# Branch products from split operands, gate inputs read back in eight transfers, and another order of VectorE's work

## The chip, the cores and the metric

One core of a Trainium2 (trn2) chip runs the whole program in one launch. The metric is the device time in microseconds (us); lower is better.

## The reference

Two layers of a block with four parallel token-mixing branches and a gated feed-forward part, over 256 context tokens and 256 latent tokens of width 1024. What matters here is the merge of the branches:

```python
def merge_branches(h, ys, w_branch, w_gate, b_gate, w_o):
    gates = jax.nn.sigmoid(h @ w_gate + b_gate)
    acc = gates[..., :D_MODEL] * (ys[0] @ w_branch[0])
    for i in range(1, N_BRANCH):
        acc = acc + gates[..., i * D_MODEL:(i + 1) * D_MODEL] * (ys[i] @ w_branch[i])
    return acc @ w_o
```

Branches 0 to 3 are a short gated convolution, neighbourhood attention, grouped-query attention and a two-pass RWKV-7 recurrence, each 256 channels wide. After the merge come an RMS norm, a residual sum, a second RMS norm with modulation, and the feed-forward part. In layer 1 only the latent tokens go through the merge and what follows.

## The kernel before

Everything is held with channels on the 128 partitions and tokens along the free axis, 512 columns (T) in layer 0 and, for most products, 256 in layer 1. A product of a weight with an activation is made by `project` (L2109): ACT rounds a weight half (1024 x 128) to fp32r (`whi`, L988), DVE takes the rest (`wlo = ring - whi`, L1472), the activation is held as a high and a low part as well, and PE makes three matmuls for each 128 rows: high x high, high x low, low x high (L2118 to L2120). The halves are made `SPLIT` = 3 ahead, in a ring of three slots for each of whi and wlo; SP's queue loads the blocks of two halves (1 MB each) into a ring of three as `lo_done` or the product frees a slot. The branch products (L2508) are the exception: they read the branch outputs `YB` and the weights `WB` as plain fp32, two matmuls for each output tile of 128 channels.

The order of PE's jobs is written out once in `job_list` (L213); each job takes the next PSUM bank in turn (`bank_plan`, L282) and waits until that bank's last user has read it. The stages of one layer in order, with the layer-0 times of the profile:

- Attention in steps of two units (to 318 us). In each step come scores, transposes, some of the gate products (branches 0 and 1, `gates_in_step`) and preparatory work of the recurrence (`first_pass`). In the step `PREP_STEP[l]["shift"]` DVE finishes three shifted copies (`shifted`, L1639) that ACT begins (L1109) at the end of its own step; DVE's `first_pass` stands ahead of its `split_until` for the step's gates.
- The two passes of the recurrence (318 to 455 us): products of small blocks, then the levels 2, 4, 8, 16, 32 of a triangular inverse, each of jobs `sx`, `tt`, `sy` (L2365, L2353, L2405) with extras (`tok` L2316, `xv` L2397), then `u0` and `at` (L2416, L2424), then a chunk loop with modulation jobs (`mod` L2165, `modt` L2173), then `y1` and `y23` (L2466, L2478, L2482). In the second pass POOL brings the gate inputs `HG` back from DRAM (L914): after `tok k` it issues two transfers of 2 MB (1 MB in layer 1), one for the high and one for the low part. At the end DVE makes three wlo halves (L1472), then adds `y1` (L1882) and `y23` (L1890) into YB.
- The merge loop (455 to 604 us). For J in 0 to 3, two output tiles j at a time, the branches go in `GATE_ORDER` = 2, 0, 1, 3; branches 2 and 3 have their gate products here (48 matmuls for the two tiles), those of 0 and 1 come back from DRAM as `GB`. The recurrence's group norm is worked in at J = 0 (`mean`, `var`, `g2`: L2499, L2515, L2521; `centred`, `readout`). POOL loads WB (1 MB for each J, two buffers, L922), GB (L927), and at J = 1 the residual stream X (L934). In layer 0 ACT squares X (`XX`) and DVE sums the squares during J = 2 and 3.
- The output product (`wo`, 604 to 649 us), 24 matmuls for each of eight tiles. Layer 0 is `FUSED`: while wo runs, ACT and DVE form squares and sums (L1960, L1963, L1968), and four `sum` jobs (L2527, L2536, L2538, L2541) give both norms at once. `sum 0` (the sum of XX) stands ahead of the last wo tile.
- The gap (649 to 663 us): four modulation jobs on PE, the roots on ACT, then for each tile on DVE `scaled_out` (L1988), `new_x` (L1993), `normed` (L1997), on ACT the modulated value (L1396) and its high part (L1400), on DVE `low` (L2001). Then `project_first` (L2127; matmuls L2141 to L2143) starts five up tiles side by side, 15 matmuls for each tile of the input as it comes.

What sets the start of the first late gate product is this part of DVE's order:

```python
if d == 1:
    split_until(half_no(("gate", l, 0, GATE_ORDER[0])) + SPLIT)
```

## Time and profile before

| what | value |
|---|---|
| median of 3 runs | 1687.19 us (1682.79 to 1688.15) |
| the profiled execution | 1686.72 us |
| its span | 1684.9 us |
| PE / PEld / DVE / ACT / POOL busy | 1603.2 / 1317.8 / 912.0 / 780.8 / 302.5 us |
| mean granted TensorE clock | 0.978 |
| bytes moved | 234.41 MB, mean 139 GB/s |

The profiled execution took 1686.72 us by the device's count, 1.8 us more than the span of its records, and lies 0.5 us under the median. PE is TensorE's matmuls, PEld its weight loads, DVE VectorE, ACT ScalarE, POOL GpSimd, SP SyncE (only DMA issues). A matmul's recorded length is modelled and overlaps the next one's, so the pace is read from start to start. PEclk 1.00 stands for 2.4 GHz and 0.50 for 1.2 GHz. "issue" is time in which an engine waited for nothing that the profile shows. An fp32 matmul has two records, an fp32r one has one.

### The profile page before, as it was taken

The page shows a single profiled execution, that of the slowest core. Times are in us where ns is not written, and L with a number is a line of the kernel's source. Part 1 is how long each engine was busy: PE and PEld are TensorE (multiplying, and loading weights), DVE is VectorE, ACT ScalarE, POOL GpSimd, SP SyncE. Part 2 cuts the span into 40 slices and gives each one's busy share as a digit, 9 for nine tenths or more (in the row PEclk, how much of TensorE's full clock was granted, in tenths as well). Part 3 has the DMA queues.
Part 4 walks back from the last instruction along what each step waited for, and adds up shares of the span by engine and source line. Part 5 has one row for each costly group of instructions (what it writes and reads, how often), then busy time and mean ns, then how long its engine had stood idle before and what let it go on. Part 6 is the DMA issues. An engine that isn't in the chain of part 4 may idle for free.

```text
span 1684.9 us, 33073 instructions
## 1 busy us (share of the span) xinstructions
PE 1603.2 (95%) x14128; PEld 1317.8 (78%) x14128; DVE 912.0 (54%) x1457; ACT 780.8 (46%) x1295; POOL 302.5 (18%) x241
## 2 busy tenths in 40 slices
PE   6999999998899999999999998999998899999997
PEld 3788767777766676888888885987876789899997
DVE  3264455564344558555554225655776356567754
ACT  4332456473343346534434225525666444566652
POOL 0160234322010000111222000211452020012201
PEclk8999999998999999999999999999999999999999
DMA  9753234233862252123324434833413384544553
GB/s 336 185 159 99 95 107 157 73 114 93 276 221 79 75 175 75 54 97 101 100 88 94 113 111 139 256 125 113 131 63 128 94 296 161 198 154 163 178 173 116
DMA packets 230497, 234.41 MB, mean 139 GB/s; under 512 B 5904, under 2 KB 217232, under 8 KB 230352
## 3 DMA queue, kind: packets, MB, share of 16 engines
q1 hardware_dynamic: 210720, 190.09, 34.7%
q0 software_dynamic: 15024, 35.92, 7.8%
q10 hardware_dynamic: 4608, 6.29, 1.1%
q8 instruction: 113, 1.85, 0.4%
q14 instruction: 32, 0.26, 0.1%
HBM read 216.55 MB, written 15.73 MB: 138 GB/s over the span
## 4 chain that ended last, share of the span: by engine, by line
PE 72%; DVE 4%; issue 2%; ACT 2%; DMA 1%; POOL 0%; ACTq 0%; DVEq 0%; POOLq 0%
PE ps L2118 17%; PE ps L2119 16%; PE ps L2120 16%; PE ps L2508 5%; PE ps L2165 2%; PE ps L2365 2%; PE ps L2353 1%; PE ps L2405 1%; PE ps L2141 1%; PE ps L2142 1%; PE ps L2143 1%; PE ps L2327 1%; PE ps L2173 1%; DVE wlo L1472 1%; PE ps L2316 1%
## 5 line engine op out<-in xcount | busy, mean ns | idle before, releaser
L988 ACT ACTIVATE whi<-ring 128x1024 fp32r<-128x1024 f32 (+1 forms) x264 | 274.9, 1045 | 512.2 <-PE ps L2120 467.8
L1472 DVE TENSOR_TENSOR wlo<-ring,whi 128x1024 fp32r<-128x1024 f32 (+1 forms) x264 | 327.4, 1245 | 182.5 <-ACT whi L988 181.9
L2118 PE MATMUL ps<-H,whi 128*128 128x256 f32 (+1 forms) x640 | 215.1, 336 | 1.9 <-DVE wlo L1472 1.8
L2120 PE MATMUL ps<-H,wlo 128*128 128x256 f32 (+1 forms) x640 | 214.9, 336 | 0.0
L2119 PE MATMUL ps<-H,whi 128*128 128x256 f32 (+1 forms) x640 | 214.8, 336 | 0.0
L2118 PE MATMUL ps<-HR,whi 128*128 128x512 f32 (+1 forms) x568 | 203.0, 357 | 3.4 <-DVE wlo L1472 3.4
L2120 PE MATMUL ps<-HR,wlo 128*128 128x512 f32 (+1 forms) x568 | 199.0, 350 | 0.0
L2119 PE MATMUL ps<-HR,whi 128*128 128x512 f32 (+1 forms) x568 | 198.9, 350 | 0.0
L2118 PEld LDWEIGHTS ps<-H,whi 128*128 128x128 f32 x640 | 122.2, 191 | 14.5 <-issue 2.2
L2120 PEld LDWEIGHTS ps<-H,wlo 128*128 128x128 f32 x640 | 122.2, 191 | 12.2
L2119 PEld LDWEIGHTS ps<-H,whi 128*128 128x128 f32 x640 | 122.3, 191 | 12.0
L2118 PEld LDWEIGHTS ps<-HR,whi 128*128 128x128 f32 x568 | 108.2, 191 | 20.7 <-issue 7.1
L2119 PEld LDWEIGHTS ps<-HR,whi 128*128 128x128 f32 x568 | 108.2, 191 | 14.3 <-issue 1.0
L2120 PEld LDWEIGHTS ps<-HR,wlo 128*128 128x128 f32 x568 | 108.2, 190 | 13.9
L886 POOL TENSOR_SCALAR pr<-pr,stat 128x512 f32<-128x512 f32 (+1 forms) x48 | 72.1, 1514 | 237.3 <-DVE stat L1744 237.3
L2118 PE MATMUL ps<-UA,whi 128*128 128x512 f32 (+1 forms) x320 | 107.6, 336 | 0.0
L2119 PE MATMUL ps<-UA,whi 128*128 128x512 f32 (+1 forms) x320 | 107.5, 336 | 0.0
L2120 PE MATMUL ps<-UA,wlo 128*128 128x512 f32 (+1 forms) x320 | 107.5, 336 | 0.0
L942 POOL TENSOR_TENSOR CU<-CU,rs 128x512 f32<-128x512 f32 (+1 forms) x22 | 39.3, 1786 | 367.8 <-ACT rs L1440 367.8
L2118 PE MATMUL ps<-HG,whi 128*128 128x512 f32 (+1 forms) x256 | 91.1, 356 | 4.5 <-DVE YB L1882 4.5
L2120 PE MATMUL ps<-HG,wlo 128*128 128x512 f32 (+1 forms) x256 | 86.8, 339 | 0.0
L2119 PE MATMUL ps<-HG,whi 128*128 128x512 f32 (+1 forms) x256 | 86.7, 339 | 0.0
(351 smaller groups left out, 3076.6 us busy)
## 6 DMA issues: line engine op xcount, KB each, us to landing
ring<-in_ffn_up SPq DMA_DIRECT2D x44, 1024.0 KB, 5.0
ring<-in_w_gate SPq DMA_DIRECT2D x32, 1024.0 KB, 5.7
ring<-in_ada_w SPq DMA_DIRECT2D x32, 1024.0 KB, 5.1
ring<-in_w_in SPq DMA_DIRECT2D x24, 1024.0 KB, 6.6
ring<-in_ffn_down SPq DMA_DIRECT2D x32, 512.0 KB, 3.7
ada<-in_ada_w SPq DMA_DIRECT2D x8, 1024.0 KB, 11.6
WB<-in_w_branch POOLq DMA_DIRECT2D x8, 1024.0 KB, 6.8
ring<-in_w_o SPq DMA_DIRECT2D x8, 1024.0 KB, 5.0
```

What stands on the lines that cost most here:

```text
L886: pool.tensor_scalar(pr[:, u % 4, 0:nk], pr[:, u % 4, 0:nk], stat[:, 2, u % 4:u % 4 + 1], None, ALU.mult).then_inc(p_ready, 1)
L942: pool.tensor_tensor(u, u, (rs, rt)[j % 2][:, c0:c1], ALU.mult).then_inc(u_ready, 1)
L988: act.activation(whi[HALF_SLOT[m]][:, 0:kn, :], ring[:, SLOT[raw] % RING, 0:kn, P * half:P * half + P], ACT.Copy).then_inc(hi_done, 1)
L1472: dve.tensor_tensor(wlo[HALF_SLOT[m]][:, 0:kn, :], ring[:, SLOT[raw] % RING, 0:kn, P * half:P * half + P], whi[HALF_SLOT[m]][:, 0:kn, :].b ...
L2118: pe.matmul(o[:, c0:c1], hi[:, i, :], part(0, k), start=(k == 0), stop=False)
L2119: pe.matmul(o[:, c0:c1], hi[:, i, :], part(1, k), start=False, stop=False)
L2120: last = pe.matmul(o[:, c0:c1], lo[:, i, :], part(0, k), start=False, stop=(k == kn - 1))
L2141: pe.matmul(o, hi[:, k, :], part(0, k)[:, c0:c1], start=(k == 0), stop=False)
L2142: pe.matmul(o, hi[:, k, :], part(1, k)[:, c0:c1], start=False, stop=False)
L2165: last = pe.matmul(o[STRIP * g:STRIP * g + STRIP, 0:SLOT_N], cpad[:, k, :], w[:, k, :], start=(k < STRIPS), stop=(k >= KT - STRIPS))
L2365: last = pe.matmul(o[side(y), x, CH2 * b:CH2 * b + CH2].rearrange("k (g n) -> k g n", n=z), LM1[side(x), 2 * p + y, b, 0:CH], even_blocks( ...
L2508: last = pe.matmul(o[:, c0:c1], wb[:, 2 * i + k, P * (j % 2):P * (j % 2) + P], YB[:, 2 * i + k, c0:c1], start=(k == 0), stop=(k == 1))
```

## The change

- The branch products of layer 0 (`BRANCH_SPLIT`) are made like the others, from high and low parts: ACT rounds branch outputs (`YH`, `source_hi`, eight of 128 x 512) and branch weights (`WH`, three slots, `branch_hi`, eight of 128 x 1024), DVE takes the low parts (`YL`, `WL`), PE makes six fp32r matmuls for a job that had two fp32 ones. `YH` lies where X is, so X is read back in four transfers behind the last branch products, and the squares of X with their sums move into the wo loop.
- The gate inputs come back in eight transfers (0.5 MB each in layer 0, 0.25 MB in layer 1), each behind another job of the second pass's levels (`GATE_INPUT_BEHIND`), in both layers.
- `sum 0` moves behind the other three sums.
- DVE: in the shift step the halves come ahead of `first_pass`; at the end of the second pass one half, `y1` of pair 0, one half, `y1` of pair 1, one half; in the layer-0 gap `normed` of the next tile stands ahead of `low`, and `low(0)` ahead of the modulation sum.
- ACT: in the layer-0 gap the row copy of the last modulation job comes behind the first tile's high part.

```diff
+SOURCE_ORDER = [2 * i + x for i in GATE_ORDER for x in range(2)]
...
+GATE_INPUT_BEHIND = [("tok", "k", 1), ("sx", 16, 1), ("tt", 16, 1), ("sy", 16, 1),
+                     ("sx", 32, 1), ("tt", 32, 1), ("sy", 32, 1), ("u0", 1)]
...
+BRANCH_SPLIT = (0,)
...
-jobs += [("wo", l, j) for j in range(7)] + [("sum", l, 0)] * (l in FUSED) + [("wo", l, 7)]
+jobs += [("wo", l, j) for j in range(8)]
 if l in FUSED:
-    jobs += [("sum", l, q) for q in range(1, 4)] + FILL.get(("gap", l, 1), []) + FILL.get(("gap", l, 2), [])
+    jobs += [("sum", l, q) for q in (1, 2, 3, 0)] + FILL.get(("gap", l, 1), []) + FILL.get(("gap", l, 2), [])
...
+YH = at("YH", 0, [KT, T], F32R)
+YL = at("YL", 16, [KT, T], F32R)
+WH = at("WH", 156, [3, KT, P], F32R)
+WL = at("WL", 112, [2, KT, SLOT_N], F32R)
...
-for part in range(2):
-    pool.dma_start(HG[:, part, :, c0:T], hsave[part, :, c0:T].rearrange("(k p) t -> p k t", p=P))\
+for n, behind in enumerate(GATE_INPUT_BEHIND):
+    pool.wait_ge(mm_done, done_at((behind[0], l, 1) + behind[1:]))
+    part, k = n // 4, n % 4 * 2
+    pool.dma_start(HG[:, part, k:k + 2, c0:T],
+                   hsave[part, P * k:P * k + 2 * P, c0:T].rearrange("(k p) t -> p k t", p=P))\
         .then_inc(h_back[l], 16)
...
-if J == 1:
...
-        if l:
-            pool.wait_ge(x_saved, 16)
-        pool.dma_start(X[:, :, c0:c1],
-                       (xsave if l else a["xin"])[:, c0:c1].rearrange("(k p) t -> p k t", p=P))\
-            .then_inc(x_back, 16)
+    if J == 1 and l not in BRANCH_SPLIT:
+        pool.wait_ge(x_saved, 16)
+        pool.dma_start(X[:, :, c0:c1], xsave[:, c0:c1].rearrange("(k p) t -> p k t", p=P))\
+            .then_inc(x_back[0], 16)
     pool.wait_ge(wb_in, 16 * (4 * l + J + 1))
+if l in BRANCH_SPLIT:
+    for i in GATE_ORDER:
+        pool.wait_ge(mm_done, done_at(("br", l, KT - 1, i)))
+        pool.dma_start(X[:, 2 * i:2 * i + 2, c0:c1],
+                       a["xin"][2 * P * i:2 * P * i + 2 * P, c0:c1].rearrange("(k p) t -> p k t", p=P))\
+            .then_inc(x_back[i], 16)
...
+def fill(point, part=slice(None)):
+    for job in [job for job in FILL.get(point, []) if job[0] == "mod"][part]:
...
+def source_hi(n):
+    act.activation(YH[:, n, c0:c1], YB[:, n, c0:c1], ACT.Copy).then_inc(yh_done, 1)
+def branch_hi(j):
+    act.wait_ge(wb_in, 16 * (4 * l + j // 2 + 1))
+    if j > 2:
+        act.wait_ge(mm_done, done_at(("br", l, j - 3, GATE_ORDER[3])))
+    act.activation(WH[:, j % 3, :, :], WB[:, j // 2 % 2, :, P * (j % 2):P * (j % 2) + P], ACT.Copy)\
+       .then_inc(wh_done, 1)
+if l in BRANCH_SPLIT:
+    act.wait_ge(ya_ready, 2 * l + 2)
+    for n in range(len(units) - NBANK, len(units)):
+        emptied(act, ("PV", l, n))
+    act.wait_ge(mm_done, done_at(("y23", l, 1, 1)))
+    for i in GATE_ORDER[:3]:
+        for n in (2 * i, 2 * i + 1):
+            source_hi(n)
...
    .then_inc(frees(("gate", l, j, i)), 1)
+if l in BRANCH_SPLIT and (j, i) == (0, GATE_ORDER[0]):
+    branch_hi(0)
+    branch_hi(1)
...
-if l in FUSED and J >= 2:
-    n = 4 * (J - 2) + GATE_ORDER.index(i)
-    if n == 0:
-        act.wait_ge(x_back, 16 * (l + 1))
-    if n > 1:
-        act.wait_ge(x2_added, 7 * FUSED.index(l) + n - 1)
-    act.activation(XX[:, min(n, 1), c0:c1], X[:, n, c0:c1], ACT.Square).then_inc(x2_ready, 1)
+if l in BRANCH_SPLIT:
+    if i == GATE_ORDER[2] and J < 3:
+        branch_hi(2 * J + 2)
+    if READOUT.get((J, i)) == "g2":
+        for p in range(2):
+            emptied(act, ("g2", l, p))
+            source_hi(6 + p)
+    if i == GATE_ORDER[3] and J < 3:
+        branch_hi(2 * J + 3)
...
 for j in range(KT):
+    act.wait_ge(x_back[j // 2], 16)
+    if j > 1:
+        act.wait_ge(x2_added, 7 * f + j - 1)
+    act.activation(XX[:, min(j, 1), c0:c1], X[:, j, c0:c1], ACT.Square).then_inc(x2_ready, 1)
     s = filled(act, ("wo", l, j))
...
-fill(("gap", l, 2))
+fill(("gap", l, 2), slice(0, 1))
...
 act.activation(H2[:, 0, i, c0:c1], OB[:, i, c0:c1], ACT.Copy).then_inc(h_hi, 1)
+if i == 0:
+    fill(("gap", l, 2), slice(1, None))
...
-first_pass(j // 2)
+shift_step = j // 2 == PREP_STEP[l]["shift"]
+if not shift_step:
+    first_pass(j // 2)
 for t in gates_in_step(l, j // 2):
     name = ("gate", l) + t
     split_until(min(half_no(name), half_no(("gate", l) + GATE_TILES[-1]) + 1 - SPLIT) + SPLIT)
+if shift_step:
+    first_pass(j // 2)
...
+first_gate = half_no(("gate", l, 0, GATE_ORDER[0]))
 if d == 1:
-    split_until(half_no(("gate", l, 0, GATE_ORDER[0])) + SPLIT)
+    split_until(first_gate + 1)
...
 ins.then_inc(frees(("y1", l, d, p)), 1)
+split_until(first_gate + p + 2)
...
+def source_lo(n):
+    dve.wait_ge(yh_done, 8 * BRANCH_SPLIT.index(l) + SOURCE_ORDER.index(n) + 1)
+    dve.tensor_tensor(YL[:, n, c0:c1], YB[:, n, c0:c1], YH[:, n, c0:c1].bitcast(F32), ALU.subtract)\
+       .then_inc(yl_done, 1)
+def branch_lo(j):
+    dve.wait_ge(wh_done, 8 * BRANCH_SPLIT.index(l) + j + 1)
+    half = slice(P * (j % 2), P * (j % 2) + P)
+    dve.tensor_tensor(WL[:, j // 2 % 2, :, half], WB[:, j // 2 % 2, :, half],
+                      WH[:, j % 3, :, :].bitcast(F32), ALU.subtract).then_inc(wl_done, 1)
+if l in BRANCH_SPLIT:
+    for n in SOURCE_ORDER[:6]:
+        source_lo(n)
+    branch_lo(0)
+    branch_lo(1)
...
-if l in FUSED and J >= 2:
-    n = 4 * (J - 2) + GATE_ORDER.index(i)
-    dve.wait_ge(x2_ready, 8 * FUSED.index(l) + n + 1)
-    if n:
-        if n > 1:
-            dve.wait_ge(x2_added, 7 * FUSED.index(l) + n - 1)
-        dve.tensor_tensor(XX[:, 0, c0:c1], XX[:, 0, c0:c1], XX[:, 1, c0:c1], ALU.add).then_inc(x2_added, 1)
+if l in BRANCH_SPLIT:
+    if READOUT.get((J, i)) == "g2":
+        for p in range(2):
+            emptied(dve, ("g2", l, p))
+            source_lo(6 + p)
+    if i == GATE_ORDER[2] and J < 3:
+        branch_lo(2 * J + 2)
+    if i == GATE_ORDER[3] and J < 3:
+        branch_lo(2 * J + 3)
...
-dve.wait_ge(x_back, 16 * (l + 1))
 for j in range(KT):
     t = tile_of_sums(j)
+    dve.wait_ge(x2_ready, 8 * f + j + 1)
+    if j:
+        if j > 1:
+            dve.wait_ge(x2_added, 7 * f + j - 1)
+        dve.tensor_tensor(XX[:, 0, c0:c1], XX[:, 0, c0:c1], XX[:, 1, c0:c1], ALU.add).then_inc(x2_added, 1)
+    dve.wait_ge(x_back[j // 2], 16)
...
 dve.wait_ge(root_ready, norm_no(l, 2) + 1)
+normed(0)
 for i in range(KT):
-    normed(i)
-    if i:
-        low(i - 1)
-    else:
+    if i + 1 < KT:
+        scaled_out(i + 1)
+        new_x(i + 1)
+        normed(i + 1)
+    low(i)
+    if i == 0:
         fill(("gap", l, 2))
-        scaled_out(1)
-    if i + 1 < KT:
-        new_x(i + 1)
-    if i + 2 < KT:
-        scaled_out(i + 2)
-low(KT - 1)
...
-pe.wait_ge(h_back[l], 32)
+pe.wait_ge(h_back[l], 128)
...
-for j in (2 * J, 2 * J + 1):
+for j in (2 * J, 2 * J + 1) if l in BRANCH_SPLIT else ():
+    o = job(("br", l, j, i))[:, c0:c1]
+    f = 8 * BRANCH_SPLIT.index(l)
+    pe.wait_ge(yl_done, f + 2 * GATE_ORDER.index(i) + 2)
+    pe.wait_ge(wl_done, f + j + 1)
+    half = slice(P * (j % 2), P * (j % 2) + P)
+    for k in (2 * i, 2 * i + 1):
+        pe.matmul(o, WH[:, j % 3, k, :], YH[:, k, c0:c1], start=(k == 2 * i), stop=False)
+        pe.matmul(o, WH[:, j % 3, k, :], YL[:, k, c0:c1], start=False, stop=False)
+        last = pe.matmul(o, WL[:, J % 2, k, half], YH[:, k, c0:c1], start=False, stop=(k > 2 * i))
+    done(last)
...
-if j == KT - 1 and l in FUSED:
-    pe.wait_ge(x2_added, 7 * (FUSED.index(l) + 1))
-    o = job(("sum", l, 0))
-    done(pe.matmul(o[:, c0:c1], K("ones"), XX[:, 0, c0:c1], start=True, stop=True))
...
+pe.wait_ge(x2_added, 7 * (f + 1))
+o = job(("sum", l, 0))[:, c0:c1]
+done(pe.matmul(o, K("ones"), XX[:, 0, c0:c1], start=True, stop=True))
```

## Rows read from the trace of the kernel before

**Rows 1.** The page: busy time of each engine.
```profile
PE 1603.2 (95%) x14128; PEld 1317.8 (78%) x14128; DVE 912.0 (54%) x1457; ACT 780.8 (46%) x1295; POOL 302.5 (18%) x241
```

**Rows 2.** The chain in layer 0's merge loop: start, length, what.
```profile
494.41 3.43 PE ps L2508 x8
508.74 10.30 PE ps L2508 x24
```

**Rows 3.** Engines in one whole J of that loop (stretch: length, busy PE, PEld, DVE, ACT, POOL, PEclk, DMA share, GB/s).
```profile
533.36:568.88 35.52, 35.52 (x130) 24.10 (x129) 16.52 (x23) 12.44 (x19) 0.89 (x1) 1.00 0.26 89
```

**Rows 4.** Groups by shape: DVE's and ACT's work on a weight half.
```profile
L1472 DVE TENSOR_TENSOR wlo<-ring,whi 128x1024 fp32r<-128x1024 f32 x248 | 312.0, 1264 | 155.2 <-ACT whi L988 154.6
L988 ACT ACTIVATE whi<-ring 128x1024 fp32r<-128x1024 f32 x248 | 261.4, 1058 | 474.1 <-PE ps L2120 438.0 <-PE ps L2143 7.1 <-PE ps L2196 6.4
```

**Rows 5.** Timeline of DVE in the wo loop, layer 0: the least idle time.
```profile
643.89 0.69 DVE L1960 TENSOR_TENSOR SQB<-X,OB 128x512 f32<-128x512 f32 x1 [0.61 <-ACT OB L1373]
```

**Rows 6.** Windows as in rows 3: levels of layer 0, gate start of layer 1.
```profile
416.00:418.00 2.00, 0.01 (x1) 0.01 (x1) 0.00 (x0) 0.00 (x0) 0.00 (x0) 1.00 1.07 317
418.00:420.00 2.00, 2.00 (x79) 1.83 (x79) 0.42 (x1) 0.60 (x1) 0.03 (x1) 0.76 0.12 32
...
422.00:424.00 2.00, 2.00 (x20) 1.67 (x23) 0.33 (x1) 0.82 (x2) 0.00 (x0) 0.50 1.01 211
...
1362.00:1364.00 2.00, 2.00 (x11) 2.00 (x11) 0.00 (x0) 0.00 (x0) 0.00 (x0) 0.50 1.08 388
```

**Rows 7.** The chain through levels 16 and 32 of the second pass, both layers.
```profile
411.84 1.29 PE ps L2365 x64
...
428.36 0.27 PE ps L2416
...
1320.70 1.05 PE ps L2365 x45
...
1326.30 0.55 PE ps L2365 x32
...
1330.13 1.93 issue
...
1334.48 1.92 PE ps L2416 x64
```

**Rows 8.** PE's first gate matmul in either layer, and the first branch products of layer 1.
```profile
456.86 0.47 PE L2118 MATMUL ps<-HG,whi 128*128 128x512 f32 x1 [1.93 <-DVE YB L1882]
1360.34 0.36 PE L2118 MATMUL ps<-HG,whi 128*128 128x256 f32 x1 [2.53 <-DVE YB L1882]
1368.68 3.45 PE ps L2508 x16
```

**Rows 9.** POOL's queue at the same place: its wait for the first WB of each layer.
```profile
462.01 0.90 POOL L922 DMA_DIRECT2D WB<-in_w_branch  x1 [4.35 <-DMA WB<-in_w_branch]
1367.34 0.89 POOL L922 DMA_DIRECT2D WB<-in_w_branch  x1 [6.80 <-DMA WB<-in_w_branch]
```

**Rows 10.** The gap of layer 0: DVE, ACT, PE's chain, and the clock.
```profile
657.57 0.69 DVE L1997 TENSOR_TENSOR OB<-X,SQB 128x512 f32<-128x512 f32 x1 [0.21 <-ACT SQB L1388]
658.90 0.38 ACT L1001 ACTIVATE mrow<-ps 128x256 f32<-128x256 f32 x1 [1.15 <-PE ps L2165]
662.02 0.68 DVE L2001 TENSOR_TENSOR H<-OB,H 128x512 fp32r<-128x512 f32 x1
662.85 0.77 PE ps L2141
666.00:668.00 2.00, 2.00 (x6) 1.61 (x5) 2.00 (x4) 1.34 (x3) 0.00 (x0) 0.50 0.00 0
668.00:670.00 2.00, 2.00 (x9) 1.57 (x9) 2.00 (x5) 1.32 (x4) 0.00 (x0) 0.95 0.00 0
```

**Rows 11.** The shift step of layer 1: timeline of PE and of DVE.
```profile
1165.16 0.36 PE L2118 MATMUL ps<-HR,whi 128*128 128x256 f32 x1 [3.09 <-DVE wlo L1472]
1161.81 0.75 DVE L1639 SCALAR_TENSOR_TENSOR lora<-Z,vec,lora 128x510 f32<-128x510 f32 x1 [3.17 <-ACT lora L1109]
```

11 lines of the change are left out of this document (7 added, 4 removed).

## The prediction

> **What bounds the kernel now.** I read the page first: PE is busy 95% of the span [rows 1]. So time can go in two ways only: less work on PE where it never waits, or shorter waits in the places where it does. The merge loop of layer 0 is of the first kind. One J takes 35.52 us, PE is busy in all of it at clock 1.00, while DVE works 16.52 and ACT 12.44 us [rows 3]. The chain there is PE alone: two branch jobs take 3.43 us [rows 2], and the 48 gate matmuls between 497.84 (494.41 + 3.43) and 508.74 take 10.90 us, 0.227 us each. The places of the second kind are four: the levels of the second pass, the first late gate product after it, the gap of layer 0, and the shift step of layer 1 [rows 6 to 8, 10, 11]. Everything else (attention apart from that step, feed-forward, layer 1's merge loop) is left as it is.
>
> **The change part by part.** The sum is made against the profiled execution's own 1686.72 us, which lies 0.5 us under the median of 1687.19; I let that half microsecond go.
>
> *Branch products, layer 0.* Now a job is two fp32 matmuls, 3.43 / 2 = 1.715 us [rows 2]. It becomes six fp32r matmuls of the gate products' shape: 6 x 0.227 = 1.36 us. There are 8 tiles x 4 branches = 32 jobs: 32 x 0.353 = 11.3 us less PE. What is added elsewhere: for each J two weight halves more on ACT (2 x 1.06 us) and on DVE (2 x 1.26 us) [rows 4], which makes DVE about 19 and ACT about 15 of the new 32.7 us, so PE hides them; cost 0 as long as order and latency allow. The late one is `branch_hi(2J+3)`, which waits for the first of the last two branch jobs of J; from there ACT 1.06, DVE's last multiplies and adds (some four of 0.69 [rows 5]) and 1.26 make about 5 us, and its reader stands behind 10.9 us of gates. At the head of the loop the sources come first (six of about 0.6 on ACT, of 0.69 on DVE), then WB, which landed at 462.0 [rows 9], then 1.06 + 1.26: the first low part is there near 464.5, and the gates and the mean keep PE until about 467. Cost 0; if WB came 3 us later, PE would stand that much. I count **-11.2**.
>
> *X and its squares.* The transfer of X leaves a busy stretch of the DMA and comes back as four of 0.5 MB behind the last branch jobs; the first squares are wanted some 14 us after the first of them is issued, and the last pair some 30 us after. Cost 0. In the wo loop DVE gets one addition of 0.69 us a tile. Its least idle time there is 0.61 us [rows 5], so it is full for two or three tiles and may end a few tenths late: the cover is nearly gone. `sum 0` takes the same 0.86 us of PE behind the other sums as ahead of the last tile; the sums that ACT and DVE wait for come earlier by that much, but ACT then waits for PE's second modulation job, whose time is the same. I count **0**, bounds -0.8 and +1.
>
> *Gate inputs.* In layer 0 PE stood in the middle of one job, where it waits for no semaphore, while DMA was full (1.07 in 416 to 418), and went on when the transfer was over (0.12 in 418 to 420); then the clock was 0.50 [rows 6]. I read this as PE's instructions coming late behind the 2 MB. From the start of `sx 16` to the start of `u0` took 428.36 - 411.84 = 16.5 us. Layer 1 has one undisturbed level, 1326.30 - 1320.70 = 5.6 us, and a last one of 8.18 us with 1.93 of the same wait in it, so 6.25 without [rows 7]: 11.9 together, a gain of 4.7 in layer 0. In layer 1 it is the 1.93 and about 0.9 of half clock in `u0` (1.92 us long), 2.8. A transfer of a quarter of the size can still hold one fetch up by a quarter of the time, so I take 4.0 and 2.5, together **-6.5**. Bounds: 0 (the fetches are as late as before) and -8. POOL issues eight instead of two and has nothing else until `y23`; the last, behind `u0`, is issued about 25 us before its reader. The Trainium skill, page "DMA: Bandwidth & Descriptors", section "Queues, rings and completion order", says that each DMA engine takes turns between the queues it has work for, a packet at a time; by that rule an instruction fetch would not wait for a whole transfer of another queue, however large, and the eight would bring nothing. The wait of [rows 6] that ended with the transfer speaks against it.
>
> *The first late gate product.* Before, DVE makes three halves and then adds `y1`, for whose bank PE waits: 1.93 us in layer 0, 2.53 in layer 1 [rows 8]. Now one half (1.26) and two additions stand ahead of it, both shorter than PE's `y23`, so PE goes straight on. Layer 0: **-1.9**. In layer 1 the 2.5 us, and some 1.7 lost to the half clock that followed (0.50 in 1362 to 1364 [rows 6]), bring PE sooner to its branch products; but WB landed at 1367.3 and the products began at 1368.68 [rows 8, 9]. More than 1.3 is not to be had, PE then stands about 2.5 us for WB, and the clock may fall again. I take **-0.5**, bounds -1.3 and +0.5.
>
> *The gap of layer 0.* `normed(0)` begins at 657.57, `low(0)` at 662.02, and PE starts at 662.85 [rows 10]. Between them stand the modulation sum and ACT's row copy at 658.90, which waits for PE and holds up the first modulated value. Afterwards: ACT starts at 658.3 (1.1 + 0.6), DVE makes three operations of 0.6 meanwhile, `low(0)` ends near 660.9, PE starts at 661.05: 1.8 less. PE then has been idle 1.7 instead of 3.5 us. It ran at 0.50 until about 668.2 (0.95 in 668 to 670), 5.4 us, and at full speed half of that, 2.7, is saved if the clock stays up. It stayed up after the idle 1.93 of layer 0's gate start and fell after the 2.53 of layer 1's [rows 6, 8]. DVE makes a tile in 4 x 0.6 = 2.4 us and PE uses one in 15 x 0.227 = 3.4, so DVE isn't late next. **-4.4**, bounds -1 and -4.6.
>
> *The shift step.* In layer 1 DVE waited 3.17 us for ACT's copies with two halves behind them, and PE 3.09 us for the first of these halves [rows 11]. Now the halves go first; ACT made the second by 1160.2, so both are ready by 1161.5, when PE wants them. DVE's later work moves by 2.1 us only (the copies themselves are no earlier), and that governs the rest of the step: **-2.3**, bounds 0 (another engine takes over) and -3.1. In layer 0 PE did not wait there: **-0.3** for less crowding on DVE.
>
> Sum: 11.2 + 6.5 + 1.9 + 0.5 + 4.4 + 2.3 + 0.3 = 27.1. 1686.7 - 27.1 = **1659.6**.
>
> **The rivals.**
> - *The transfers do not matter.* The stalls stay (by whatever cause, the page's turn-taking among them). Then 6.5 is missing: 1666. For it: similar waits named "issue" are seen without traffic. Against: the end of the wait with the end of the transfer.
> - *The clock takes part back.* It falls in the gap of layer 0 all the same (+2.7) and while PE waits for WB in layer 1 (+1): 1663. Speaking for it: the light modulation jobs ahead of the gap; against: the 1.93 us that did no harm.
> - *The split branch products are fed late.* The first pair waits for WB, ACT, DVE, or each J waits for the half behind the last branch job, 2 to 3 us each: about 1669. Against it stand the 5 us of margin worked out above.
> - *The change doesn't do what it says.* The fp32r branch matmuls keep a pace of 0.29 us (1.715 / 6), as they alternate between tiles of several buffers: 1671. No row shows this, every fp32r product here runs at 0.227.
> - *Slower: each small transfer stalls PE.* If a transfer of any size cost a stall of about 2.9 us, as the one in layer 0 did, then 16 transfers instead of four would mean up to 12 stalls more, 35 us, in the levels of both layers, and the 6.5 would not come either: 1686.7 - 20.6 + 35 = 1701. It decides from about seven more stalls on. Against it: one of the two transfers of layer 0 did nothing of the sort.
>
> **How the numbers follow.** Forecast 0.52, clock 0.16, transfers 0.14, fed late 0.08, not as it says 0.03, slower 0.03, and 0.04 for several terms falling short together (about 1675). About 0.3% (5 us) is what a measurement of this kernel can tell from no change; all cases but one lie well under 1682, so faster 0.95, same 0.02, slower 0.03. The range goes up to 1671, over the first four cases. Down, if all terms reached their bounds (0.8 + 1.5 + 0.8 + 0.2 + 0.8), it would be 1655.5; new overlap in places that I have not priced takes it to 1652.
>
> **What would show it.** Layer 0's J should take 32.7 us with L2508 gone from it and matmuls of WH, WL at 0.227. No idle time of PE within one job in levels 16 and 32, clock 1.00 there; `sx 16` to `u0` near 12 us. PE's first HG matmul directly behind `y23` in both layers; in layer 1 a wait for WB ahead of the first L2508. PEclk 1.00 from the first H2 matmul on. No wait of 3 us in layer 1's shift step. I am wrong on the main term if a J takes over 34 us; wrong on the transfers if waits called issue of over 1 us stand in the middle of a job.

## The result, and the profile after

| kernel | median | runs | ratio to before, 95% interval |
|---|---|---|---|
| before | 1686.2 us | 4 (1682.79 to 1688.15) | |
| changed, first comparison | 1668.95 us | 4 (1663.82 to 1778.68) | 0.988 [0.985, 0.9911] |
| before, repeated | 1689.06 us | 17 (1684.0 to 1700.02) | |
| changed, repeated | 1667.7 us | 6 (1663.49 to 1682.34) | 0.9877 [0.9838, 0.9915] |

The changed kernel is about 1.2% faster. The forecast was 1659.6 us with 1652 to 1671 around it: the sign and the range hold, the point lies 8 to 9 us too low. The profile read here is that of the repeat, because in the first profile of the changed kernel, the run of 1778.68 us, TensorE had only 0.85 of its clock. The execution of the repeat's profile took 1670.02 us, its span 1668.2 us: 16.7 less than the span of before.

In the changed kernel the branch products are L2585 to L2587 (layer 0) and L2592 (layer 1), the fp32r products of `project` L2191 to L2193, of `project_first` L2214 to L2216, a level's `sx`, `tt`, `sy` L2438, L2426, L2478.

The page, engine times as in [rows 1], and one row of its queue part (packets, MB, share of 16 engines) that will matter:

```profile
PE 1589.0 (95%) x14192; PEld 1325.5 (79%) x14192; DVE 926.5 (56%) x1473; ACT 792.3 (47%) x1311; POOL 312.5 (19%) x256
...
q8 instruction: 114, 1.87, 0.5%
```

PE's busy time is 14.2 us shorter. The second row is PE's program itself: it is read in packets of 16 KB while the kernel runs.

Windows, columns as in [rows 3]: a whole J of layer 0, the levels, the chunk loop behind them, the gap.

```profile
525.14:557.78 32.64, 32.64 (x145) 27.04 (x144) 17.38 (x23) 12.17 (x17) 0.88 (x1) 1.00 0.29 97
416.00:418.00 2.00, 0.59 (x9) 0.56 (x10) 0.23 (x1) 0.00 (x0) 0.00 (x0) 0.96 0.96 237
418.00:420.00 2.00, 2.00 (x28) 1.67 (x30) 0.20 (x1) 1.08 (x2) 0.93 (x2) 0.50 0.37 82
440.00:442.00 2.00, 0.98 (x16) 0.42 (x16) 0.37 (x2) 0.00 (x0) 0.00 (x0) 0.93 1.08 366
442.00:444.00 2.00, 2.00 (x24) 1.64 (x20) 0.29 (x1) 0.38 (x1) 0.00 (x0) 0.50 1.08 376
648.00:650.00 2.00, 2.00 (x6) 1.61 (x5) 1.95 (x4) 0.96 (x3) 0.00 (x0) 0.50 0.04 8
```

J takes 32.64 us where [rows 3] had 35.52, and PE is full in it. But the levels still have their hole (416 to 418) with the half clock behind it, and two more things go against the forecast: half clock in the chunk loop, where before ran at 1.00, and half clock after the gap.

PE's timeline at the places of [rows 6, 8, 10] and in the chunk loop (start, length, what, idle time before it and what ended it):

```profile
417.40 0.31 PE L2438 MATMUL ps<-TN,LM 64*64 64x32 f32 x6 [2.16 <-issue]
437.01 1.07 PE L2238 MATMUL ps<-ring,cpad 128*32 128x256 f32 x16 [0.34 <-DMA ring<-in_ada_w]
441.02 1.29 PE L2238 MATMUL ps<-ring,cpad 128*32 128x256 f32 x16 [1.41 <-DMA ring<-in_ada_w]
647.39 0.77 PE L2214 MATMUL ps<-H,whi 128*128 128x512 f32 x1 [1.89 <-DVE H L2077]
1341.02 0.36 PE L2191 MATMUL ps<-HG,whi 128*128 128x256 f32 x1 [0.33 <-DVE wlo L1519]
1350.50 0.92 PE L2592 MATMUL ps<-YB,WB 128*128 128x256 f32 x3 [2.64 <-DMA WB<-in_w_branch]
```

The wait of 2.94 us inside a job has become 2.16. The modulation jobs of the chunk loop (L2238) wait for their weights, which they did nowhere in this loop before. The idle time of the gap went from 3.48 to 1.89. The first late gate product of layer 1 follows at once (2.53 before), and PE waits 2.64 for WB ahead of the first branch product, as forecast (2.5).

DVE in the shift step of layer 1, where before had the 3.17 us of [rows 11]: the halves come first.

```profile
1145.20 1.22 DVE L1519 TENSOR_TENSOR wlo<-ring,whi 128x1024 fp32r<-128x1024 f32 x1 [0.46 <-ACT whi L1006]
1146.75 0.75 DVE L1686 SCALAR_TENSOR_TENSOR lora<-Z,vec,lora 128x510 f32<-128x510 f32 x1 [0.33 <-ACT lora L1127]
```

Since both kernels issue nearly the same matmuls in the same order, each can be matched with its own in the other trace; the difference of the start times, read at the borders of the stages, splits the 16.7 us:

```
stage (times of before)                        forecast   measured
start, attention, first pass (0 to 399)          -0.3       -2.8   (shift step of layer 0: -1.1; clock about -1.1)
second pass, layer 0 (399 to 454)                -4.0       +2.3
first late gate product, layer 0                 -1.9       -1.9
merge loop, layer 0 (457 to 605)                -11.2      -11.4
wo and gap, layer 0 (605 to 672)                 -4.4       -1.4
shift step, layer 1                              -2.3       -2.6
rest of attention and both passes, layer 1       -2.5       +0.6
gate start to first branch product, layer 1      -0.5       -0.9
everything behind it, and feed-forward              0       +1.3
```

The row of layer 1's gate start begins at the end of `y23`. Four stages are close to the forecast: the merge loop, the shift step and both gate starts. Three are not: the second pass of layer 0, the passes of layer 1 (together +2.9 for a forecast of -6.5) and the gap. Two more moved by more than any term stood for: the start (half a microsecond of it lies in the first 30 us, and no run says why) and the end.

### The profile page after: what moved, and what is told of

Its sections match the earlier page's. It is cut to its first block, busy times and chain, and to the rows that moved or that the text cites. A ratio compares the mean times of both kernels' runs of the same rounds, so it can differ in the third digit from the quotient of the medians.

```text
span 1776.9 us, 33301 instructions
## 1 busy us (share of the span) xinstructions
PE 1711.0 (96%) x14192; PEld 1364.4 (77%) x14192; DVE 931.9 (52%) x1473; ACT 793.7 (45%) x1311; POOL 312.0 (18%) x256
## 3 DMA queue, kind: packets, MB, share of 16 engines
q1 hardware_dynamic: 210720, 190.09, 33.1%
## 4 chain that ended last, share of the span: by engine, by line
PE 90%; DVE 4%; ACT 2%; issue 2%; DMA 2%; POOL 0%; ACTq 0%; SPq 0%; DVEq 0%
PE ps L2191 20%; PE ps L2192 20%; PE ps L2193 20%; PE ps L2238 2%; PE ps L2592 2%; PE ps L2426 1%; PE ps L2438 1%; PE ps L2348 1%; PE ps L2378 1%; PE ps L2356 1%; PE ps L2214 1%; PE ps L2478 1%; PE ps L2215 1%; PE ps L2216 1%; PE ps L2246 1%
## 5 line engine op out<-in xcount | busy, mean ns | idle before, releaser
L2191 PE MATMUL ps<-H,whi 128*128 128x256 f32 (+1 forms) x640 | 224.2, 350 | 1.8 <-DVE wlo L1519 1.8
L2192 PE MATMUL ps<-H,whi 128*128 128x256 f32 (+1 forms) x640 | 224.1, 350 | 0.0
L2193 PE MATMUL ps<-H,wlo 128*128 128x256 f32 (+1 forms) x640 | 223.1, 349 | 0.0
L2191 PE MATMUL ps<-HR,whi 128*128 128x512 f32 (+1 forms) x568 | 213.7, 376 | 0.0
L2192 PE MATMUL ps<-HR,whi 128*128 128x512 f32 (+1 forms) x568 | 209.6, 369 | 0.0
L2193 PE MATMUL ps<-HR,wlo 128*128 128x512 f32 (+1 forms) x568 | 209.5, 369 | 0.0
L2191 PEld LDWEIGHTS ps<-H,whi 128*128 128x128 f32 x640 | 123.6, 193 | 20.7 <-issue 2.2
L2193 PEld LDWEIGHTS ps<-H,wlo 128*128 128x128 f32 x640 | 123.9, 194 | 18.4
L2191 PEld LDWEIGHTS ps<-HR,whi 128*128 128x128 f32 x568 | 110.2, 194 | 24.3 <-issue 4.0
L2193 PEld LDWEIGHTS ps<-HR,wlo 128*128 128x128 f32 x568 | 110.6, 195 | 20.7
L2192 PEld LDWEIGHTS ps<-HR,whi 128*128 128x128 f32 x568 | 110.1, 194 | 20.8 <-issue 0.9
L2191 PE MATMUL ps<-UA,whi 128*128 128x512 f32 (+1 forms) x320 | 112.3, 351 | 0.2 <-DVE wlo L1519 0.2
L2192 PE MATMUL ps<-UA,whi 128*128 128x512 f32 (+1 forms) x320 | 112.3, 351 | 0.0
L2193 PE MATMUL ps<-UA,wlo 128*128 128x512 f32 (+1 forms) x320 | 111.7, 349 | 0.0
L2191 PE MATMUL ps<-HG,whi 128*128 128x512 f32 (+1 forms) x256 | 92.8, 363 | 1.1 <-DVE YB L1934 0.9
L2193 PE MATMUL ps<-HG,wlo 128*128 128x512 f32 (+1 forms) x256 | 90.6, 354 | 0.0
L2192 PE MATMUL ps<-HG,whi 128*128 128x512 f32 (+1 forms) x256 | 90.4, 353 | 0.0
```

The costliest lines, as they stand in the source:

```text
L2191: pe.matmul(o[:, c0:c1], hi[:, i, :], part(0, k), start=(k == 0), stop=False)
L2192: pe.matmul(o[:, c0:c1], hi[:, i, :], part(1, k), start=False, stop=False)
L2193: last = pe.matmul(o[:, c0:c1], lo[:, i, :], part(0, k), start=False, stop=(k == kn - 1))
```

## The experiments

All compare with the kernel before, run on the same chip in the same comparison (its median was 1686.1 to 1691.1). Single runs of one kernel mostly differ by 5 to 10 us, some by up to 19, and the slower ones have mostly the lower mean clock, so the totals are coarse and the matched stages carry the argument.

### e1, the changed kernel again

No edit.

> The changed kernel again, for a profile at a full clock. Measured was a gain of about 17 to 20 us, where the sum said 27.1. Theory A (one term failed whole, the rest stand): a J of layer 0's merge loop takes 32.7 us and the missing 7 to 10 us lie in the stretch of the levels (sx 16 to u0 still about 16.5 us in layer 0), or in the gap (first H2 matmul late, PEclk 0.50). Theory B (the products fell short): a J takes over 34 us, with PE waiting for WH or WL. Theory C (all terms came, and new waits took the rest): each place shows its gain and PE stands somewhere new for 7 us or more.

1667.7 us (0.9877 [0.9838, 0.9915]); its profile is the one read above. Part of each theory came: a J takes 32.64 us, so B is out; `sx 16` to `u0` (15.0 us) and the gap fell short, as A has it, and the waits for modulation weights are new, as C has it.

### e2, two transfers again

```diff
-for n, behind in enumerate(GATE_INPUT_BEHIND):
-    ...
+pool.wait_ge(mm_done, done_at(("tok", l, 1, "k", 1)))
+for part in range(2):
+    pool.dma_start(HG[:, part, :, c0:T], hsave[part, :, c0:T]...)
```

> The changed kernel with the gate inputs back in two transfers, as before. My theory: 6.5 us slower than the changed kernel (4.0 in layer 0, 2.5 in layer 1), with PE standing 2 to 3 us within one job at levels 16 or 32 and the clock at 0.50 behind it. Rival (the transfers do not matter): within 1 us of the changed kernel, with the same waits at the same places. Second rival (eight transfers cost something): faster than the changed kernel.

1672.0 us (0.9895 [0.9861, 0.9929]). In layer 0 the stretch from `sx 16` to `u0` takes 15.9 us (16.5 before, 15.0 in e1), and from the start of level 4 to the end of `y23` it takes 55.4 (55.3 before): the eight transfers gain one microsecond in the levels, and in the profile above lose more behind them. (The recorded expectations call this stretch "level 8 to y23"; by the matched matmuls it begins at level 4 in layer 0, and in layer 1 at the `bon` products ahead of level 2.) The waits inside a job that my theory named are there (2.40 us in layer 0, 2.23 and 2.03 in layer 1, by the counts below); the median is 4.3 us over e1's, with intervals that overlap. In layer 1, though, `bon` to `u0` takes 38.6 us, where the kernel before, with the same two transfers, took 32.0. Something other than the transfers has made layer 1 worse by 6.6 us.

### e3, plain branch products

```diff
-BRANCH_SPLIT = (0,)
+BRANCH_SPLIT = ()
...
+pool.dma_start(X[:, :, c0:c1], (xsave if l else a["xin"])[:, c0:c1]...).then_inc(x_back[0], 16)
```

> The changed kernel with layer 0's branch products in plain fp32 again, X read back at J = 1 as before (its squares stay in the wo loop). My theory: 11.2 us slower than the changed kernel, a J at 35.5 us against 32.7. Rival (the split products are fed late): less than 8 us slower, and the changed kernel shows waits of PE for wl_done or yl_done in the merge loop.

1674.77 us (0.9913 [0.9878, 0.9947]). The merge loop of layer 0 is back to the time of before (difference 0.0, where e1 has -11.4). That is the whole of the term, shown. Yet the total rises by 7.1 only, and layer 1's second pass offers a reason: `bon` to `u0` takes 29.9 us here, against 33.0 in e1, and up to the end of `y23` the difference is 3.8, as e1 waits 1.49 us more inside `y23`. So the split products, all of them in layer 0, seem to cost layer 1 some 3 us; e9 tests it.

### e4, the old orders

DVE's and ACT's orders of before in the shift step, at the end of the second pass and in the gap; products and transfers as changed.

```diff
-shift_step = j // 2 == PREP_STEP[l]["shift"]
+shift_step = False
...
-split_until(first_gate + 1)
+split_until(first_gate + SPLIT)
...
-    split_until(first_gate + p + 2)
...
-fill(("gap", l, 2), slice(0, 1))
+fill(("gap", l, 2))
```

> The changed kernel with all three orders of VectorE and that of ScalarE's row copy as before; products and transfers stay changed. My theory: 9.4 us slower (gate starts 2.4, gap 4.4, shift step 2.6), PE waiting again 1.9 and 2.5 us for y1, 3.1 us in layer 1's shift step, and 3.5 us ahead of the first H2 matmul. Rival (what an order gives is taken back by the next wait, WB in layer 1, POOL or ACT in attention, the clock in the gap): 3 to 5 us slower only.

1679.43 us (0.9942 [0.9921, 0.9963]), 11.7 above e1. By stage against e1: layer 0's shift step 1.1, its gate start 1.3, its gap 0.9, layer 1's shift step 2.6; layer 1 from `y23` to the first branch product the same (-1.0 here, -0.9 in e1), since WB sets that. That is 6; the rest of the difference of the medians is in no stage that the orders touch (the profiled executions differ by 4.2). So the stages are nearer to the rival than to the 9.4: WB takes layer 1's gate start back, and the half clock, which stands in both kernels, most of the gap.

### What a wait called issue is

In all runs so far I counted the records of PE's queue (matmuls, weight loads and semaphore instructions) up to each wait of over 1 us that ends with "issue" in the middle of a job. The recorded expectation of e6 names matmuls and weight loads alone; the counts come out with the semaphore instructions among them.

```
kernel   count of PE's records where it waited (wait, us)        modulo 256
before   8385 (2.94)  9921 (1.34)  22977 (1.93)                  193 each
e1       8641 (2.16)  22977 (1.18)  24257 (1.49)                 193 each
e2       6849 (1.07)  8385 (2.40)  8897 (1.42)  22721 (2.23)  22977 (2.03)  24257 (1.49)   193 each
e3       8641 (2.44)                                             193
e4       6849 (1.07)  8641 (2.16)  22977 (1.45)  24257 (1.49)    193 each
```

256 instructions are one packet of q8: 114 packets for some 29,000 instructions. So PE waits at the border of a block. The trace of before shows the block itself: DMA by queue around the moment at which PE crossed the border ahead of it (411.2), and from the fetch on.

```profile
DMA packets 580, 1.19 MB, mean 201 GB/s; under 512 B 0, under 2 KB 0, under 8 KB 580
q0 software_dynamic: 580, 1.19, 81.1%
...
q0 software_dynamic: 434, 0.86, 109.5%
q8 instruction: 1, 0.02, 2.5%
```

The first two rows are 409.5 to 415.4, with no packet of q8; the other two 415.4 to 418. From the packet records: when PE crosses one border, the block that begins at the next one is fetched. In every wait of the table PE went on 1.2 to 1.5 us after the last fetch before it had ended. In the levels with no gate input traffic (e8 below) the fetch begins 0.8 to 1.3 us after the crossing and lasts 0.9 to 1.3; at a border where PE had to wait 0.93 us it went on 3.85 us after the last crossing, so the levels would need it in 2.9. Behind 2 MB the fetch began 4.3 us after the crossing (411.18 to 415.45), in e1, with 0.5 MB transfers, 2.6 us (412.41 to 415.04). In either case the traffic was still going on when the fetch began: in before it ended at 416.5, PE went on at 417.99, and the 2 MB transfer landed at 419.6 only.

### e5, PE kept busy in layer 0's gap

```diff
 outs = [job(name, n) for n, name in enumerate(names)]
+if names[0][0] == "up" and names[0][1] in (0,):
+    for _ in range(2):
+        pe.matmul(outs[0][:, c0:c1], K("ones"), XX[:, 0, c0:c1], start=True, stop=True)
```

> Two more fp32 products of 128x512 (two records and 0.86 us each) stand on PE behind the last modulation job of layer 0's gap, into the bank that the first up tile then starts anew; nothing reads them. In the changed kernel PE was idle 1.89 us there and the next 6.8 us went at the half clock. Theory A (the clock falls because PE does nothing for those 1.9 us on top of the light modulation jobs): with the idle time filled the clock stays at 1.00, the first 15 products of the first tile are paced at 0.23 us in place of 0.43, and the stage is some 3 us shorter. Rival B (the light modulation jobs before it, or the step to full load after it, bring the clock down whatever PE does in those 1.9 us): the clock falls all the same, the stage is no shorter (0 to +0.2 us), and the half clock stands at the same place.

1661.36 us (0.987 [0.9836, 0.9903]). Windows and PE's timeline of this kernel:

```profile
645.00:647.00 2.00, 2.00 (x12) 1.12 (x8) 1.82 (x4) 1.97 (x5) 0.00 (x0) 1.00 0.02 4
647.00:649.00 2.00, 1.93 (x9) 1.24 (x8) 1.93 (x6) 1.56 (x3) 0.00 (x0) 1.00 0.03 8
...
645.51 1.96 PE L2207 MATMUL ps<-XX,con 128*128 128x512 f32 x4
647.55 0.47 PE L2219 MATMUL ps<-H,whi 128*128 128x512 f32 x1
```

The clock stays at 1.00, and from the first product of `project_first` to the last of its first tile PE gains 2.8 us over e1. So theory A: without the idle 1.89 us the clock does not fall, and that is worth the 2.7 us that I had estimated. Whether the same idle time behind heavier work would have brought it down, no run shows.

### e6, other block borders

The first `sx` group of layer 0's first pass is issued twice:

```diff
-for b, x, y in corners():
+for b, x, y in list(corners()) * (2 if (l, d, n, p) == (0, 0, 0, 0) else 1):
```

> One group of 64 small matmuls of the first pass of layer 0 (the first sx of level 2) is issued twice, 128 PE instructions and about 1.3 us more; nothing else changes. In the runs so far every wait of PE called issue in the middle of a job stands at the same count of PE's instructions modulo 256 (193 by my count of matmul and weight-load records; 256 instructions fill one 16384-byte packet of the instruction queue). Theory A (PE's instructions come in blocks of 16 KB, and a wait is a block that comes late): in this kernel the waits in the levels again stand at 193 modulo 256 by the whole count, so in the code 64 matmuls earlier than in the changed kernel or at another block, and never at the old places in the code (matmul 4190 of the changed kernel, now 4254; 10656, 10781, 11157, now 64 more). Rival B (the wait belongs to the job or to the moment of a transfer): the waits stand at the same places in the code, so 64 matmuls later by count. Time: 1.3 us longer by the doubled group, plus or minus 3 by which blocks come late.

The group turned out to have 16 products of two matmul records and two weight loads each, 64 records in place of 128, so the code moved by a quarter of a block. 1668.31 us (0.989 [0.9853, 0.9927]). Every wait called issue of over 0.7 us in the middle of a job stands at 193 modulo 256 of the whole count again, 6849 (1.21), 8641 (3.08), 9921 (1.15), 10177 (1.24) and 22721 (1.31) among them, though the code at these counts is now that which stood 64 records earlier in e1. Theory A holds: the wait belongs to the border, not to the job.

### e7, points spread more evenly

```diff
-("sx", 16, 1), ("tt", 16, 1), ("sy", 16, 1), ("sx", 32, 1), ("tt", 32, 1), ("sy", 32, 1), ("u0", 1)
+("sx", 16, 0), ("tt", 16, 1), ("sy", 16, 1), ("sx", 32, 0), ("tt", 32, 1), ("sy", 32, 0), ("tt", 64, 1)
```

> The eight transfers stand behind points spread more evenly and ending earlier: tok k; sx 16 of the first pair; tt 16; sy 16; sx 32 of the first pair; tt 32; sy 32 of the first pair; tt 64. In the changed kernel two of them came 1.0 us apart (behind sx 16 and tt 16), and the last, behind u0 at 428 us, was still moving when the weights of the chunk loop's modulation jobs were issued at 430. Theory A (stretches of traffic longer than the time PE takes for one block of instructions make a wait; the last transfer makes the modulation weights late): layer 0's levels show no wait called issue over 1 us, PE does not wait for these weights in the chunk loop, no half clock there, and this stage is 2 to 5 us shorter than in the changed kernel. Rival B (any traffic at the moment of a fetch can hold it up, and the modulation weights are late because PE and SP are earlier, not because of the last transfer): a wait of about 2 us stays at some block, and PE still waits 1 us or more in the chunk loop.

1669.52 us (0.9902 [0.9871, 0.9933]). One half of each theory: the levels keep a wait of 2.44 us at the same border (`sx 16` to `u0` 15.3 us), but PE does not wait for the modulation weights, and from the start of the chunk loop to the end of `y23` it takes 21.7 us, against 26.8 in e1. Windows of e7 over that loop:

```profile
438.00:442.00 4.00, 4.00 (x76) 3.10 (x72) 1.60 (x6) 0.77 (x2) 0.00 (x0) 1.00 1.08 382
442.00:446.00 4.00, 4.00 (x78) 2.62 (x76) 1.82 (x7) 0.58 (x2) 0.00 (x0) 1.00 1.09 380
```

### e8, no gate input traffic in the levels

```diff
-GATE_INPUT_BEHIND = [("tok", "k", 1), ...]
+GATE_INPUT_BEHIND = [("u0", 1)] * 8
```

> All eight transfers stand behind u0 in both layers, so the levels of the second pass see no gate input traffic at all. Theory A (the waits called issue in the levels come from this traffic): no such wait in levels 8 to 32 of either layer, from the start of level 16 to u0 about 11.5 us in layer 0 (16.5 before) and clock 1.00 there; the 4 MB then collide with the modulation weights (3 MB) and the first halves' weights (4 MB): PE waits 4 to 10 us in layer 0's chunk loop or at the first late gate product, so the whole is slower than the changed kernel by 0 to 8 us. Rival B (the waits come from elsewhere): the levels keep a wait of 2 us or so without the traffic.

1678.2 us (0.9936 [0.9909, 0.9962]). `sx 16` to `u0` takes 11.8 us in layer 0: the 11.9 that I had taken from layer 1 as its undisturbed time was right. What is left of the wait, in PE's timeline, and the price behind it:

```profile
412.23 0.31 PE L2437 MATMUL ps<-TN,LM 64*64 64x32 f32 x6 [0.93 <-issue]
435.94 1.94 PE L2237 MATMUL ps<-ring,cpad 128*32 128x256 f32 x16 [5.49 <-DMA ring<-in_ada_w]
```

Even with no gate input traffic a fetch is 0.93 us late at that border. The modulation weights come 5.49 us late, and from 1.3 us into this wait on the clock is at 0.50 for 20.5 us.

### e9, layer 1's block borders near those of before the change

```diff
-for b, x, y in corners():
+for b, x, y in (list(corners())[:24] if (l, d, n) == (1, 0, 0) else []) + list(corners()):
```

> In layer 1's first pass the first 24 small matmuls of either sx group of level 2 are issued twice: 48 matmuls with their weight loads, 96 PE instructions, some 0.9 us. The split branch products of layer 0 put 160 PE records more in front of layer 1; 160 + 96 = 256, so the 16 KB blocks of PE's instructions begin again where they did before the change. Theory A (the split products cost layer 1's second pass some 4 us by moving these borders: from level 8 to y23 it took 54.8 us before and 51.7 with plain products, both with the old borders, but 55.3 to 57.3 in the three other kernels with the eight transfers and the new ones): this stretch takes 51 to 53 us, and the whole is 2 to 3 us under the changed kernel. Rival B (chance from run to run, or the traffic alone): 55 to 57 us as in the changed kernel, and the whole 1 us slower.

1661.46 us (0.9846 [0.9816, 0.9877]). The edit does not do quite what the expectation says. `corners()` has 16 entries, so `[:24]` takes all of them, and each is four records: 128 records were added, not 96, and 160 + 128 = 288 leaves the borders 32 records off their old places in the code. (By the same count they stand 60 off in e11 and 40 off in e12 below.) They are near those of before, not on them. From `bon` to the end of `y23` of layer 1, by matched matmuls, it takes 53.7 us, a little over the 51 to 53 expected and 1.8 under e1. Up to `u0`, by how far the borders stand from those of before:

```
off by   layer 1, bon to u0 (us)
0        e3 29.9    before (two transfers) 32.0
32       e9 30.8
40       e12 31.5
60       e11 30.7
160      e1 33.0    e4 34.7    two transfers (e2) 38.6
160      other points (e7) 36.8    sixteen (e10) 36.9    no traffic (e8) 33.1
168      e5 33.3
224      e6 31.0
```

With the changed kernel's own transfers in layer 1, the five kernels with their borders off by 0 to 60 or by 224 take 29.9 to 31.5 us, the three off by 160 or 168 take 33.0 to 34.7. Where the borders fall is worth some 3 us here, more than the traffic (e8 without any takes 33.1). The place off by 160, which the split products brought, is the bad one, and theory A holds in this form. The whole is 0.3% under e1 by the ratios, with intervals that overlap.

### e10, sixteen transfers

Each of 0.25 MB, behind one job of levels 16 and 32 each, then `tt 64` and `u0`.

```diff
-part, k = n // 4, n % 4 * 2
-pool.dma_start(HG[:, part, k:k + 2, c0:T], ...)
+part, k = n // 8, n % 8
+pool.dma_start(HG[:, part, k:k + 1, c0:T], ...)
```

> Sixteen transfers of a half size (0.25 MB in layer 0), each behind one job of levels 16 and 32 (both pairs), tt 64 and u0 of the first pair. In layer 0 the stretch from the first sx 16 to u0 took 16.5 us before, 15.9 with two transfers, 14.9, 14.9, 14.9 and 15.5 with eight, 15.3 with eight more evenly placed, 11.7 with none. Theory A (a fetch is held up by as much as its queue has before it, so smaller transfers hold it up less): 13 us or less, no wait of over 1 us. Rival B (the bytes moved in the stretch decide, or one transfer of any size holds a fetch up): 14.9 to 15.5 as with eight. In the chunk loop PE waits less than 1 us for the modulation weights, as the last transfer is smaller and 1 us earlier.

1667.84 us (0.9898 [0.9861, 0.9934]). `sx 16` to `u0` takes 12.9 us, as theory A has it, though one wait of 2.02 us is left. PE does not wait for the modulation weights, as expected. But the time saved was lost at once. PE's timeline and windows:

```profile
426.99 0.45 PE L2521 MATMUL ps<-X 64*64 64x64 f32 x8 [1.79 <-issue]
428.26 0.45 PE L2513 MATMUL ps<-state,AT 64*64 64x64 f32 x8 [0.59 <-DVE state L1910]
...
432.00:436.00 4.00, 4.00 (x44) 2.49 (x43) 1.07 (x4) 0.39 (x1) 0.00 (x0) 0.50 0.75 239
452.00:456.00 4.00, 4.00 (x59) 3.53 (x56) 1.35 (x4) 3.22 (x4) 0.00 (x0) 0.50 0.67 220
```

PE waited 1.79 us at a later border (9153), ahead of the light chunk loop, and in this profile nearly the whole loop then ran at half clock: 33.4 us, where before took 21.6. The median of its runs is 10 us under the profiled one (1678.37), so perhaps this does not always happen.

### e11 and e12, the parts together

e11 has PE kept busy in layer 0's gap, at the layer boundary and in layer 1's gap, the borders near those of before, as in e9, and, in layer 0, the points of e7; e12 is e11 without the two later busy places.

```diff
+BUSY = {("up", 0): (2, 512), ("z", 1): (7, 512), ("up", 1): (2, 256)}   # e12: ("up", 0) alone
...
+if names[0][:2] in BUSY:
+    count_, width = BUSY[names[0][:2]]
+    for _ in range(count_):
+        pe.matmul(outs[0][:, 0:width], K("ones"), con[:, 0:width], start=True, stop=True)
```

> The changed kernel with four additions: products that nobody reads keep PE busy while it waits in layer 0's gap (two of 512 columns), at the layer boundary (seven of 512) and in layer 1's gap (two of 256); 30 small matmuls of layer 1's first pass are issued twice, which with the 36 records of the first two places brings the borders of PE's instruction blocks back to those of before (36 + 60 = 96 records, as in the kernel with the borders restored); and layer 0's gate inputs stand behind the evenly spread points. Theory A (all of these are stalls or half clocks of their own): no half clock at the three places, which cost 3.4, 3.4 and about 2 us in the changed kernel, some 3 us less in layer 1's second pass, and no wait for modulation weights in layer 0's chunk loop: 1655 to 1659 us. Rival B (the clock of the layer boundary and of layer 1's gap is set by what comes before and after, and only layer 0's gap can be saved): about 1662.

> The kernel before this one without the products that kept PE busy at the layer boundary and in layer 1's gap: left are the two products in layer 0's gap, the restored block borders (44 small matmuls of layer 1's first pass issued twice, 88 + 8 = 96 records) and the evenly spread transfers in layer 0. Theory A (layer boundary and layer 1's gap give nothing: there the half clock of 6.8 us at the boundary cost 0.6 us only, as the first products wait for VectorE's tiles anyway, and in layer 1's gap a half clock stood in spite of the products; layer 0's gap gives 2.8 and the borders 2 to 3): 1656 to 1660 us, not over the 1658.5 of that kernel by more than 2. Rival B (keeping PE busy at the layer boundary matters more than its stage shows): 1661 to 1663 us.

e11 takes 1658.51 us (0.9844 [0.9818, 0.987]), e12 1658.08 (0.9816 [0.9768, 0.9864]). Both are faster than the kernel before. By the ratios e11 is 0.3% and e12 0.6% under the changed kernel (0.9877 [0.9838, 0.9915]), with intervals that overlap, so that they beat it too is likely and not shown. At the layer boundary 6.8 us of half clock disappeared and the stage gained 0.6; in layer 1's gap half clock stood all the same. e12 without them is as fast. So e11's time is the one that its theory A named, but one of its terms failed (layer 1's gap) and one gave little; e12 bears out its theory A. In both, PE has no wait for modulation weights of over 0.3 us, and the chunk loop of layer 0 takes 22.0 and 21.7 us. Windows of e11:

```profile
434.00:438.00 4.00, 4.00 (x71) 2.74 (x70) 2.05 (x8) 0.38 (x1) 0.00 (x0) 1.00 0.94 305
438.00:442.00 4.00, 4.00 (x74) 3.04 (x72) 1.45 (x7) 0.77 (x2) 0.00 (x0) 1.00 1.09 382
```

## Why the prediction was right, and where it was wrong

**Branch products: right, but not all of their cost was in the sum.** J at 32.64 for 32.7, the merge loop -11.4 for -11.2, no wait in the feed of the split halves; X and its squares cost nothing. The step I did not take was to count the instructions added: 160 records more in front of layer 1 move every block border behind them by five eighths of a block. That cost some 3 us in layer 1's second pass (e3, and the eight kernels compared in e9). I had said that every stage other than the four named was left as it is; for a stage bounded by the fetch of instructions that is not so when the count ahead of it changes.

**Gate inputs in eight: that fetches wait was right, the step "a quarter of the size can still hold one fetch up by a quarter of the time" was wrong.** PE did wait for instructions, and the undisturbed stretch is 11.8 us (estimate 11.9). But the kernels with eight transfers at these points and the borders of layer 0 unmoved (e1, e3, e4, e5, e9) keep 2.2 to 2.4 us of the 2.94: the fetch, about 1 us after the crossing without traffic, began 4.3 us after it behind 2 MB and still 2.6 behind half-megabyte transfers, so half of the delay stayed. In e1 `sx 16` to `u0` went from 16.5 to 15.0, not to 12.5. Wrong too was the reading that the wait ended with the transfer: the fetch began in the midst of it, and PE went on 1.6 us before it landed. The Trainium skill, page "DMA: Bandwidth & Descriptors", section "Queues, rings and completion order", has each engine take turns between queues by packets; by that rule neither size should hold the fetch for long. The fetch did come in the midst of a transfer, as the rule has it, but its 4.3 and 2.6 us are more than the rule alone explains; what held it up no record shows.

The second half of the miss is what came next, the transfers' tail. The last one, behind `u0` at 427.95 us, ran into the modulation weights issued from 430.14; PE waited 1.41 us for them and the light loop went on at half clock. In these five profiles (e1, e3, e4, e5, e9) level 4 to the end of `y23` took 57.5, 53.6, 55.5, 58.0 and 58.8 us, against 55.3 and 55.4 with two transfers. On average that is a loss of 1.3 us in layer 0, within a spread of 5 from profile to profile; the gain of 4.0 that I had forecast is in none of them. The rival "the transfers do not matter" (1666) named the right time, for another reason: they mattered, and it was given back. That the tail makes the weights late is shown: the first of them took 6.5 to 7.5 us from issue to landing in the six kernels in which the last transfer was still moving (e1, e3, e4, e5, e6, e9), and 4.9 to 5.1 in the six in which it had landed (before, e2, e7, e11, e12) or was a small one that landed within 1 us (e10). What PE loses by it varies: 1.0 to 1.5 us and a half clock in e1, e4 and e5, but 0.5 us at most and no half clock from it in e3, e6 and e9. In e7, e11 and e12, where the last transfer is earlier, this loop takes 21.7 to 22.0 (22.0 in e3 too). It is not the only cause: in e9 the same loop fell to half clock without such a wait, behind 1.5 us at a border. In layer 1 with the old borders (e3 against before) both passes behind the shift step took 3.1 us less, for a forecast of 2.5.

**First late gate product: right in both layers.** -1.9 for -1.9, and in layer 1 WB took the place of DVE as forecast: e4, with the old order, is as fast there. Layer 1's first branch product gained 0.9 us over the end of `y23`, for a forecast of 0.5.

**The gap: the start was right, the clock was wrong.** Idle 1.89 us (forecast 1.7), 1.6 less than before for a forecast of 1.8. But "stays up" failed: I had compared with the idle 1.93 us of layer 0's gate start, after which the clock stayed at 1.00. Here 1.89 us were enough to bring it down; that the gap's light modulation jobs ahead of it matter is argued, not shown. The rival with the clock had this, at 2.7; e5 measured 2.8.

**The shift step: right** in layer 1 (-2.6 for -2.3), undersized in layer 0 (-1.1 for -0.3, where one wait of 0.8 us for a POOL result went too).

Two parts of the 16.7 no term stood for. Before 399 us about 1.1 us is less half clock (10.2 us of it from 373 us on, 13.7 before). Behind layer 1's branch products 1.3 us are lost, not by the clock, which stands at 0.50 for 6.8 us there in both kernels, but by a longer wait for the weights in layer 1's gap (1.28 us for 0.74) and short ones for DVE's halves (0.3 us each). The range held with some luck: without those 1.1 us and the half microsecond at the start the profiled 1670.0 would have been 1671.6, over the upper bound, though the medians would still have been inside. Open is how much of each run's 5 to 10 us of spread comes from which of these places, since each kernel has one profile.

## What to carry to other kernels

A wait called "issue" in the middle of a job can be the program itself arriving late: count the engine's instructions up to it, and if the counts agree modulo one packet of the instruction queue, the stage is bounded by fetches, and traffic in it, its size, and even how many instructions stand ahead of it have a price. Follow a moved transfer to its last byte and ask what is issued there next. An idle microsecond or two can be paid again at half clock, and two idle-time products that nobody reads can be cheaper.
